# Low part of a weight tile written over its raw tile, and the load's wait moved to the slot's last matmul

## What is computed

```python
# first block
h = rmsnorm(x, norm1_gain)
q_a, f_a, i_a, g_a, q_b, k_b, v_b, f_b = split(h @ w_in)
x = x + concat([hgrn2_mixer(...), fox_mixer(...)]) @ w_out
h = rmsnorm(x, norm2_gain)
x = x + (silu(conv3(h @ w_gate)) * (h @ w_up)) @ w_down      # d_ff 5632
x = rmsnorm(x, final_norm_gain)
# second block, twice: u = h @ w_in_2[l]; pool branch (l=0) or block attention (l=1);
# attention into 256 memory tokens; y = mixed @ w_out_2[l]; h = layer_norm(alpha*h + y)
```

## Time and profile before

| | us |
|---|---|
| median of 3 runs | 2321.94 |
| span of the profiled execution | 2320.2 |
| PE busy (share of the span) | 2157.7 (93%) |
| DVE busy | 1121.2 (48%) |
| ACT busy | 925.6 (40%) |
| HBM read | 365.39 MB, 159 GB/s over the span |

### The profile page before, as it was taken

The page is one execution under the profiler, slowest core; times in us unless marked ns, Lnnn a source line. Parts: engine busy times, 40 slices in busy tenths (PEclk is TensorE's granted clock), DMA queues, the critical chain, the costliest instruction groups (busy, mean ns, idle before and its releaser), DMA issues.

```text
span 2320.2 us, 40622 instructions
## 1 busy us (share of the span) xinstructions
PE 2157.7 (93%) x17363; PEld 2131.9 (92%) x17363; DVE 1121.2 (48%) x1020; ACT 925.6 (40%) x866; POOL 31.0 (1%) x51
## 2 busy tenths in 40 slices
PE   6999999966979999999999998999798899999796
PEld 6999999965979999999999998999697899999795
DVE  3543433454465555445555455556464533454553
ACT  4433333444345554333343433334442333344431
POOL 1000000000000000000000000000000100000001
PEclk9999999978989999999999999999999999999997
DMA  7565555501535655665555566455264455545340
GB/s 253 169 199 181 179 183 182 181 1 37 181 121 172 193 174 173 176 196 189 183 183 182 152 183 183 146 182 171 78 213 138 145 181 181 163 130 164 116 134 36
DMA packets 405821, 370.54 MB, mean 160 GB/s; under 512 B 6303, under 2 KB 404444, under 8 KB 404476
## 3 DMA queue, kind: packets, MB, share of 16 engines
q1 hardware_dynamic: 405099, 365.35, 50.7%
q0 software_dynamic: 656, 4.26, 0.5%
HBM read 365.39 MB, written 4.19 MB: 159 GB/s over the span
## 4 chain that ended last, share of the span: by engine, by line
PE 89%; DVE 5%; ACT 2%; issue 1%; DMA 1%; SPq 1%; POOL 0%; POOLq 0%; DVEq 0%; ACTq 0%
PE G L370 84%; PE SB L564 2%; PE TB L462 1%; DVE xres L519 1%; PE OB L585 1%; DMA xtok<-in_x 0%; DVE al L524 0%; DMA raw<-in_w_out 0%; ACT hi L299 0%; DVE arena L441 0%; POOL xres L503 0%; PE G L852 0%; SPq L280 0%; DVE nmax L628 0%; PE OB L588 0%
## 5 line engine op out<-in xcount | busy, mean ns | idle before, releaser
L370 PE MATMUL G<-ah,hi 128*128 128x256 f32 x4032 | 1147.7, 285 | 55.5 <-DVE al L524 33.4
L370 PE MATMUL G<-al,hi 128*128 128x256 f32 x4032 | 1145.4, 284 | 0.0
L370 PE MATMUL G<-ah,lo 128*128 128x256 f32 x4032 | 1145.2, 284 | 0.0
L302 DVE TENSOR_TENSOR lo<-raw,hi 128x2048 fp32r<-128x2048 f32 (+2 forms) x372 | 776.0, 2118 | 662.6 <-ACT hi L299 662.6
L370 PEld LDWEIGHTS G<-ah,hi 128*128 128x128 f32 x4032 | 778.8, 193 | 58.4 <-issue 58.4
L370 PEld LDWEIGHTS G<-al,hi 128*128 128x128 f32 x4032 | 778.8, 193 | 0.0
L370 PEld LDWEIGHTS G<-ah,lo 128*128 128x128 f32 x4032 | 778.5, 193 | 0.0
L299 ACT ACTIVATE hi<-raw 128x2048 fp32r<-128x2048 f32 (+2 forms) x372 | 646.3, 1771 | 286.6 <-PE G L370 271.3
L370 PE MATMUL G<-hh,hi 128*128 128x256 f32 x704 | 199.4, 283 | 2.6 <-DVE hl L1260 2.6
L370 PE MATMUL G<-hl,hi 128*128 128x256 f32 x704 | 199.2, 283 | 0.0
L370 PE MATMUL G<-hh,lo 128*128 128x256 f32 x704 | 199.2, 283 | 0.0
(11 more groups left out here) (272 smaller groups left out, 1473.2 us busy)
## 6 DMA issues: line engine op xcount, KB each, us to landing
raw<-in_w_in SPq DMA_DIRECT2D x120, 1024.0 KB, 5.7
raw<-in_w_out SPq DMA_DIRECT2D x48, 1024.0 KB, 6.7
raw<-in_w_ffn_gate SPq DMA_DIRECT2D x44, 1024.0 KB, 5.3
raw<-in_w_ffn_up SPq DMA_DIRECT2D x44, 1024.0 KB, 5.3
raw<-in_w_ffn_down SPq DMA_DIRECT2D x64, 704.0 KB, 4.9
raw<-in_w_kv_shared SPq DMA_DIRECT2D x24, 1024.0 KB, 5.8
raw<-in_w_mem_kv SPq DMA_DIRECT2D x16, 1024.0 KB, 7.1
raw<-in_pool_w SPq DMA_DIRECT2D x12, 192.0 KB, 2.6
```

Source lines behind the costliest of these rows:

```text
L302: eng.tensor_tensor(sized(lo, s, p.size), sized(raw, s, p.size), sized(hi, s, p.size).bitcast(F32), ALU.subtract).then_inc(lo_ready, 1)
L370: last = eng.matmul(G[:, bank, 0:256], l_, r_, start=st and r == 0, stop=sp and r == 2)
```

## The change

The buffer `lo` is laid at the address of `raw`: `lo` of a slot takes the place of the raw tile of the same slot, which DVE reads for the last time in the very instruction that writes `lo`. So SP may not load tile n when the `lo` of tile n-4 has been made, but only when PE has read it: the wait before a load is now on `tile_used`. 32 KiB a partition (64 to 96 of the laid-out area) are no longer used; nothing is put there. No instruction is added or taken away, and the order on every engine is as before.

```diff
         raw = at("raw", 0, [P, 4, SLOT])
         hi = at("hi", 32, [P, 4, SLOT], F32R)
-        lo = at("lo", 64, [P, 4, SLOT], F32R)
+        lo = at("lo", 0, [P, 4, SLOT], F32R)
@@ sp_phase, body
                     n = i * p.tpb + (p.tile0 + j)
-                    tile_wait(eng, lo_ready, n - 3)
+                    tile_wait(eng, tile_used, n - 3)
                     src = p.source(i, j)
                     dst = sized(raw, j % 4, p.size).rearrange("p (t n) -> p t n", t=src.shape[1])
                     eng.dma_start(dst, src).then_inc(raw_loaded[j % 4], 16)
```

## The result

| | before | after |
|---|---|---|
| median (range), us | 2321.70 (2321.33 to 2322.35), 4 runs | 2342.33 (2339.72 to 2346.30), 4 runs |
| span of the profiled execution | 2320.2 | 2337.5 |

After by before is 1.0092, with a 95% interval of 1.0078 to 1.0106: the change costs 20.6 us, where +16.2 was predicted. The ratio on the 2321.94 us that the prediction started from makes 2343.3, just above the top of its range (2342.5). The direction and the four places are those predicted; the size is short by 4.4 us. The same kernel measured again (experiment 1) gave 2340.09, so that the shortfall itself lies between 2 and 4.4 us.

What follows compares the result with a forecast made beforehand. PE, busy 93% of 2320.2 us, bounds the kernel; cost arises where engines stand behind late splits. Hand-offs 10.0 + clock 3.0 + norm 2.0 + out0 1.2 = +16.2 us: 2321.94 to 2338.1, range 2333.5 to 2342.5.

Steps and rivals of the forecast that it cites:

- the four places: Both ffn-to-down hand-offs (+5.0 us each), the clock behind them (+1.5 each), down1 to norm (+2.0), pool to out0 (+1.2).
- The steady stream: Middle of phases: 0 us, as PE's three tiles (17.3 us) cover landing and splits (9.9); w_down 11.9 against 8.0.
- Down1 to norm 2: End of down1: in0_branch's tile 1 split comes late ahead of the last eviction, +2.0 us, bounds +1.5 to +3.
- Pool to out0: Out0's tile 0 load waits for PE's tile 8 of pool, issued 1.2 us later: +1.2 us, bounds +0.8 to +2.5.
- The norms behind out and out0: Last evictions of out and out0, where a norm begins: covered with 1.6 us spare, so 0.
- The second hand-off's wait: Second ffn-to-down passage: down's tile 3 load is asked for only after the last ffn tile, +5.0 us.
- The clock after these stalls: +1.5 us each: Behind both ffn-to-down hand-offs: PE's clock falls after 6.2 us idle, +1.5 to +2.7 us each, 1.5 taken.
- one landing for both hand-offs: Down's tile 3 load at both ffn-to-down passages: 4.9 us to land; 4.7 to 5.9 gives +9.6 to +12 together.
- The clock holds: Rival: the clock stays up through 6 us of idleness at the hand-offs; +13.2 us, 2335.1; chance 0.15.
- More evictions come late: Rival: landings of 7 us or more use up spare at two norms and in0_gate; +20 us, 2342; chance 0.14.
- Transfers get better: Rival: loads no longer bunch, so `xtok` and out0's tile 1 land sooner; 2330.5 if all came; chance 0.06.
- Not slower: Rival: down's tile 3 load released a tile sooner, or change without effect; 2322 us; chance 0.05, of which 0.02 faster.

Runs made afterwards that it cites:

- experiment 1: The kernel after, unchanged, measured again: 2340.09 us, ratio 1.0079 to before.
- experiment 2: The kernel after with `lo` back at its own address, the later load wait kept: 2341.42 us, ratio 1.0086.
- experiment 8: The kernel after with each load held back one tile more (mem_k0 keeps its count): 2417.33 us, one run.
- Experiment 7: The kernel after with 50 filler matmuls (float32r, 128x256) in each ffn-to-down hand-off's wait: 2336.37 us, ratio 1.0068.
- 5: The kernel after with the last eviction moved ahead of down's fourth split at both hand-offs and of in0_branch's second split: 2324.85 us, ratio 1.0013.
- 11: The kernel after with evictions moved ahead of splits at both hand-offs, norm 2 and pool to out0 (tiles 0 and 1): 2324.14 us, ratio 1.0008.
- 10: The kernel after, evictions moved ahead at hand-offs and norm 2, F32 fillers in waits ahead of out, ffn0, in0_branch, kvs_k, in1_gate: 2352.51 us, ratio 1.0130.
- 13: The kernel after, evictions moved ahead at hand-offs, norm 2 and pool to out0, with about half the F32 fillers of 10: 2312.78 us, ratio 0.9965.
- 4: The kernel after with 42 filler matmuls (float32r, 128x256) in each ffn-to-down hand-off's wait: 2336.17 us, ratio 1.0073.
- 6: The kernel before with evictions moved ahead of splits at both hand-offs and norm 2: 2322.64 us, ratio 1.0000.
- experiment 3: The kernel after with the last ffn eviction moved ahead of the split of down's fourth tile at both hand-offs: 2324.91 us, ratio 1.0013.
- 9: The kernel before, evictions moved ahead at hand-offs and norm 2, F32 fillers in waits ahead of out, ffn0, in0_branch, kvs_k, in1_gate: 2351.97 us, ratio 1.0127.

## Why the prediction came out too low

**What held.** No instruction got slower, and the write in place costs nothing (experiment 2). The steady stream kept its cover (experiment 8). The places were the four named, with one more. Down1 to norm 2 was 2.0 for 2.0, and `xres` follows `lo` at once, as the timeline of DVE after shows against the earlier trace rows:

```profile
1453.02 2.29 DVE L302 TENSOR_TENSOR lo<-raw,hi 128x2048 fp32r<-128x2048 f32 x1 [1.68 <-ACT hi L299]
1455.23 0.68 DVE L413 TENSOR_TENSOR xres<-xres,G 128x512 f32<-128x512 f32 x1
```

Pool to out0 was 1.5 for 1.2: the wait ahead of tile 0 grew by 1.5. That tile 0 itself took 0.8 us longer at the lower clock cost nothing, since the wait ahead of tile 1 became shorter by as much. The norms behind out and out0 kept their length (the wait ahead of ffn0 is 14.43 us in both traces). The second hand-off's wait grew by 4.9 for 5.0.

**What failed: the step "The clock after these stalls: +1.5 us each".** The mechanism was right, the size was not: it is +2.1 and +2.2. I had both ends, 1.5 and 2.7, and took the lower because the wait ahead of out0 was the nearest in length. The traces give no such rule of length. Experiment 1 has the longest wait, 7.87 us, with the smallest cost, 1.5; its second, of 6.09, cost 2.0, and experiment 2's, of 7.74 and 6.41, cost 1.9 and 2.1. And tile 0 of ffn0, behind a norm of the same length each time, took 7.93 to 8.50 us in the traces of before, after and experiments 1 to 7. So the term had to stand as a range of 1.5 to 2.7, and its lower end was the wrong choice. Matmuls start 0.21 us apart at the lower level and 0.12 at the upper, 0.09 us more for each; the tiles behind the hand-offs have 21 and 23 such matmuls of 33. Experiment 7 measures the term by itself: both tiles go to 4.05 us. This is 1.3 us of the error (0.5 in experiment 1, 0.9 in experiment 2).

**What failed: one landing for both hand-offs.** The first hand-off's load lands in 5.90 us, and in 6.10 to 6.47 in the other four traces of kernels with this hand-off order; the second's in 4.69 to 5.29. The prediction took 4.9, the median, for both. With 5.9 as the first its term is 6.0; the bound stood in the text, the sum did not use it. This is 1.0 us (1.6 in experiment 1).

What goes with the slow landing stands in the traces. While the first hand-off's load is under way, a packet of 16 KB moves on a queue for instructions (q8), and none while the second's is. The DMA queues in after, in the time of the one load and of the other (packets, MB, share of 16 engines):

```profile
q1 hardware_dynamic: 1673, 0.85, 54.9%
q8 instruction: 1, 0.02, 1.3%
```

```profile
q1 hardware_dynamic: 1424, 0.72, 52.5%
```

In the eight traces with later loads in which such a packet meets the first hand-off's load (after and experiments 1 to 5, 7 and 11), it lands in 5.75 to 6.48 us; in experiments 10 and 13, where none does, in 4.66 and 4.74. Of the 600 loads of tiles 2 to 31 of both down phases in these ten traces, the 517 without a packet all land within 5.20 us, and the 18 that take longer all have one; the other 65 that have one land as soon as the rest. So the packet goes with the slow landing. No run moves it on purpose, so that it is the cause is not shown.

The Trainium skill (DMA: Bandwidth & Descriptors, "Anatomy of one DMA") gives an estimate of 3.7 us for 704 KB, by a fit to DMAs that GpSimd issues; these loads are SP's, and they take longer, 4.7 to 6.5 us at the hand-offs.

**What was missing: tile 0 of in1_gate, +1.5.** The sum put nothing there. PE waits 2.87 us ahead of it in the traces of before and after alike, yet the clock fell in after, and not in before. It fell in seven of the ten traces in which nothing was put there and the loads were not delayed further: in after and experiments 1, 2, 4, 5, 6 and 11, of which 6 has the loads of before; not in before, 3 and 7. So it comes without the later load too, and I can't say what decides it. It is a term that differs by trace: in after it stood on the dear side, in before's profiled execution on the cheap side. By that much the comparison of these two traces is luck.

1.3, 1.0 and 1.5 make 3.8 of the 4.0 us between the 16.2 predicted and the 20.2 of the stretch; the rest are terms of 0.1 to 0.3 with either sign. In experiment 1 the stretch grows by only 18.0, since out and ffn0 began with shorter tiles there; the first landing was 1.6 us above the prediction in it, and in1_gate again +1.5.

**The rivals.** *The clock holds* is out: it fell at both hand-offs in each of after and experiments 1 and 2, and when it was held (7) the stretch was still 16.1 us up. *More evictions come late* named nearly the right time (2342), in part by luck: that the clock cost more than 1.5 was right. Its other half, late evictions at norms 1 and 3 and in in0_gate, did not come: single loads landed in 5.1 to 5.4 us, not 7. *Transfers get better* came in size (w_out 5.4 for 6.7) and not in effect: out0's second load still took 7.50 us, for 7.84. *Not slower* is out by experiment 3: a release a tile sooner would have left nothing to gain there.

**The clock, further.** The Trainium skill (TensorE: Matmul & The Clock Gate, "Loop structure matters more than you think") says that PE, where it waits for a DMA ahead of each step of a loop, starts each step cold. At the hand-offs the traces agree: behind waits of 6.1 to 7.9 us the tile begins at the lower level (mean clock 0.59 to 0.70), and with the wait filled or gone (experiments 7 and 3) it runs at 2.4 GHz. The price of a wait that lowers the clock is 1.3 to 2.7 us here in the tile behind it. It costs time only where PE doesn't wait again ahead of the next tile, as it does in out0 and kvs_k.

**Still open.** Which of the waits of 2.5 to 3 us lowers the clock in a given execution, and why the stretch of attention (457 to 563 us) varies by up to 3.2 us between traces whose code there is the same. Both may be why the runs of one kernel range over 4 to 11 us, more than the terms of 1 to 2 us that experiments 5, 6 and 11 were to show; those rest on the traces alone.

## What to carry to other kernels

When a buffer's release moves from its last writer to its last reader, don't ask only whether the loads of the steady stream still arrive in time: look for each place where something urgent (an eviction, the first step of a norm) is queued behind the split of a tile whose slot has only just come free, and move it ahead. Price the wait that results as landing plus what follows it, with the slowest landing seen at such a place, and add the lower clock of the work behind it. And where PE must wait anyway, filler matmuls that end just before the wait does gave back 1.5 to 2.7 us at three waits here. First look whether PE waits again right behind the tile: at kvs_k it did, and they cost 1.5. Priced wrongly (experiments 9 and 10) they cost 30 us.

## What the runs showed of the hardware

- A 128x128 by 128x256 matmul of plain F32 stands as two records of 0.22 us, 0.44 us in all, where one of float32r takes 0.12 us at the same clock (50 in 6.16 us, experiment 7).
- A wait of 2.87 us (2.71 in the profile's brackets) lowered the clock behind it in seven of ten traces and cost 1.5 us; waits of 1.4 and 1.6 us behind fillers did not, one of some 2.5 us did (experiments 7 and 4).
- At the lower level matmuls of 128x128 by 128x256 in float32r start 0.21 us apart, at the upper 0.12.
- w_down loads (704 KB, issued singly) landed within 5.20 us in 517 cases of 517 without an instruction packet (q8) beside them; with one, 65 of 83 did, and 18 took 5.29 to 6.48.
- A load of 1024 KB issued alone lands in 5.1 to 5.4 us (medians of w_ffn_gate and w_out in after); the second of two issued close together, tile 1 of out0, took 7.50 us in after and 7.84 before.
- A tensor_tensor of DVE that writes over its own operand takes what one with a separate output takes: 2121 ns in the mean over its 372 instructions both ways (after, and experiment 2).
